# Dot products over gathered expert rows: the token operand read from an SBUF copy instead of PSUM

## The reference, cut to what matters

```python
def block(args):                       # a block of 128 tokens
    xb, ib, gb = args
    ug = expert_u[ib]                  # (128 tokens, 128 picks, 1024)
    act = jax.nn.gelu(jnp.einsum("td,tkd->tk", xb, ug)) * gb
    vg = expert_v[ib]
    return jnp.einsum("tk,tkd->td", act, vg)
out = lax.map(block, (nf.reshape(4, 128, d), idx..., gates...))
```

## Time and profile before

| | |
|---|---|
| time, median of 3 runs | 3375.94 us (3371.97 to 3378.84) |
| span of the profiled execution | 3379.1 us |
| mean granted TensorE clock | 0.910 |
| PE busy | 2796.1 us, 83% |
| POOL busy | 2040.5 us, 60% |
| DVE busy | 1395.5 us, 41% |
| ScalarE busy | 646.1 us, 19% |
| HBM read | 717.02 MB |
| software (POOL-issued) DMA queue | 587.27 MB |

### The profile page before, as it was taken

How to read it: one execution, slowest core, us unless ns; L and a number is a source line. 1 busy time by engine, 2 the same in 40 slices (tenths; PEclk the granted TensorE clock), 3 DMA queues, 4 the chain that set the end, 5 groups by cost and what they waited for, 6 DMA issues and landing times.

```text
span 3379.1 us, 27308 instructions
## 1 busy us (share of the span) xinstructions
PE 2796.1 (83%) x8913; PEld 1653.4 (49%) x8913; DVE 1395.5 (41%) x2949; ACT 646.1 (19%) x1281; POOL 2040.5 (60%) x1452
## 2 busy tenths in 40 slices
PE   7358989877777777777778699899999768899997
PEld 5234534333223323333333366568878534668876
DVE  3631565666666666666524511421110326221111
ACT  3020222221111111111112311411110323121101
POOL 4886366677777677767748683135555283345652
PEclk9688999998999899989989798899999897899999
DMA  2043599999999999999984252013322250123221
GB/s 96 31 143 99 211 369 355 375 409 399 409 409 409 392 409 409 409 388 409 409 316 155 76 174 75 25 62 99 99 89 86 70 166 33 38 75 99 95 95 59
DMA packets 294802, 720.36 MB, mean 213 GB/s; under 512 B 24821, under 2 KB 149667, under 8 KB 294707
## 3 DMA queue, kind: packets, MB, share of 16 engines
q0 software_dynamic: 160512, 587.27, 44.8%
q1 hardware_dynamic: 134194, 131.92, 12.2%
HBM read 717.02 MB, written 2.10 MB: 213 GB/s over the span
## 4 chain that ended last, share of the span: by engine, by line
PE 60%; DMA 12%; POOL 12%; DVE 7%; issue 6%; ACT 3%; DVEq 0%; ACTq 0%; SPq 0%; POOLq 0%
PE ps L731 11%; PE ps L553 9%; PE ps L556 9%; PE ps L560 9%; DMA arena<-in_expert_u_dram,arena 8%; POOL arena L1110 7%; PE ps L504 5%; PE ps L697 3%; PE ps L603 3%; POOL work L1110 2%; PE ps L826 2%; POOL whi_in L1080 2%; PE ps L515 2%; DMA arena<-in_expert_v_dram,arena 1%; DVE nT L1597 1%
## 5 line engine op out<-in xcount | busy, mean ns | idle before, releaser
L731 PE MATMUL ps<-arena 128*128 128x512 f32 x1536 | 767.6, 646 | 248.7 <-ACT arena L1337 164.0
L731 PEld LDWEIGHTS ps<-arena 128*128 128x128 f32 x1536 | 304.6, 206 | 690.6 <-issue 556.7
L1864 DVE CUSTOM_DVE_ANT_0 arena<-arena,ps 128x1024 f32<-128x1024 f32 x384 | 467.5, 1219 | 304.4 <-DMA arena<-in_expert_u_dram,arena 295.4
L1110 POOL DMA_INDIRECT arena<-in_expert_v_dram,arena x384 | 360.4, 939 | 194.9 <-PE ps L731 103.4
L1110 POOL DMA_INDIRECT arena<-in_expert_u_dram,arena x384 | 362.3, 944 | 147.2 <-issue 100.0
L1080 POOL TENSOR_SCALAR whi_f<-wring 128x2048 fp32r<-128x2048 f32 (+1 forms) x60 | 125.4, 2089 | 329.7 <-DMA wring<-in_ffn_w_in_dram 202.8
L1084 POOL TENSOR_TENSOR wlo<-wring,whi_f 128x2048 fp32r<-128x2048 f32 (+1 forms) x60 | 302.1, 5035 | 11.0 <-POOL whi_f L1080 11.0
L731 PE MATMUL ps<-work,arena 128*128 128x512 f32 x512 | 240.2, 602 | 28.5 <-DMA work<-in_expert_v_dram,arena 28.5
L556 PE MATMUL ps<-n_hi,wlo 128*128 128x512 f32 x1024 | 259.3, 396 | 3.6 <-POOL wlo L1084 3.5
L556 PEld LDWEIGHTS ps<-n_hi,wlo 128*128 128x128 f32 x1024 | 196.0, 192 | 48.1 <-POOL wlo L1084 6.0
L2046 DVE TENSOR_TENSOR arena<-ps,arena 128x512 f32 x44 | 30.4, 692 | 408.0 <-PE ps L560 408.0
(11 more groups left out here) (290 smaller groups left out, 3747.1 us busy)
## 6 DMA issues: line engine op xcount, KB each, us to landing
arena<-in_ada_w_dram POOLq DMA_DIRECT2D x48, 1024.0 KB, 6.0
wring<-in_ffn_w_in_dram SPq DMA_DIRECT2D x44, 1024.0 KB, 5.1
wring<-in_ffn_w_out_dram SPq DMA_DIRECT2D x16, 1408.0 KB, 6.2
wring<-in_gla_w_in_dram SPq DMA_DIRECT2D x12, 1024.0 KB, 5.4
wring<-in_w_in_dram SPq DMA_DIRECT2D x9, 1024.0 KB, 5.1
wring<-in_w_q_dram SPq DMA_DIRECT2D x8, 1024.0 KB, 9.7
arena<-in_expert_u_dram,arena POOLq DMA_INDIRECT x384, 9.8
arena<-in_expert_v_dram,arena POOLq DMA_INDIRECT x384, 9.9
```

The source lines that it names most:

```text
L731: mm = e.matmul(ps[:, 6 + q, :], diag[:, k, :], slot_of(s)[:, q * 512:(q + 1) * 512], start=(n % HEADS == 0 and k == 0), stop=last)
L1110: e.indirect_dma_start(slot_of(seq), None, table, bass.IndirectOffsetOnAxis(ap=idx_flat[:, n * TOPK + k:n * TOPK + k + 1], axis=0)).then_i ...
L1864: inc(e.tensor_tensor_reduce(slot_of(s), slot_of(s), ps[:, 4:6, :].rearrange("p a k -> p (a k)"), 1.0, 0.0, ALU.mult, ALU.add, dots[:, n % ...
```

## The change

`tokens(t)` of PE is now followed by a step of the same name on ScalarE: one activation (Copy) of 128x1024 from PSUM banks 4 and 5 into `row[:, 0:2, :]`. It waits for the transposes (new semaphore `x_turned`) and, from block 1 on, for the last dot of the block before (`u_used` at 128 t), and its end is `x_ready`. ScalarE does it for block 0 behind the first scores, and for the later blocks behind the gelu of the last unit of the block before. PE's transposes wait only for the copy before them (`x_ready` at t). The dots read `row` in SBUF in place of PSUM. There are still 512 dots and 32 transposes; four copies are new.

```diff
             def tokens(t):                       # PE
                 if t:
-                    need("u_used", PER_BLOCK * t)
+                    need("x_ready", t)
                 for k in range(DC):
                     mm = e.transpose(ps[:, 4 + k // 4, (k % 4) * P:(k % 4 + 1) * P], nT[:, k, t * P:(t + 1) * P], ident[:])
-                inc(mm, "x_ready")
+                inc(mm, "x_turned")
...
+            def tokens(t):                       # ScalarE
+
+                need("x_turned", t + 1)
+                if t:
+                    need("u_used", PER_BLOCK * t)
+                inc(e.activation(row[:, 0:2, :].rearrange("p a k -> p (a k)"), ps[:, 4:6, :].rearrange("p a k -> p (a k)"),
+                                 ACT.Copy), "x_ready")
+
             for h in range(WQ_FIRST):
                 wq_evac(h)
                 sc_evac(h)
+                if h == 0:
+                    tokens(0)
                 if h % 2:
                     gate_exp(h // 2)
             for n in range(UNITS):
                 if n + AHEAD < UNITS:
                     gate_exp(n + AHEAD)
                 hidden(n)
+                if n % HEADS == HEADS - 1 and n < UNITS - 1:
+                    tokens(n // HEADS + 1)
                 diagonals(n)
...
                 e.wait_ge(row_landed[s % RING], 16 * (s // RING + 1))      # DVE, u_row
-                inc(e.tensor_tensor_reduce(slot_of(s), slot_of(s), ps[:, 4:6, :].rearrange("p a k -> p (a k)"), 1.0, 0.0,
+                inc(e.tensor_tensor_reduce(slot_of(s), slot_of(s), row[:, 0:2, :].rearrange("p a k -> p (a k)"), 1.0, 0.0,
                                            ALU.mult, ALU.add, dots[:, n % 2, k:k + 1]), "u_used")
```

More of the change, by code:

```diff
@@ L88 @@
         "rot_done rope_read rope_ready angle_ready trig_ready att_s att_m att_p att_n att_t att_pt  att_o att_oh "
-        "att_oe fin_t fin_ready out_done glr_in hid_ready ada_ch ada_cols gr_ready go_chunk norm_chunk nhi_ready nlo_ready w_hi w_lo hid_raw hid_hi_ready").split()
+        "att_oe fin_t fin_ready out_done glr_in hid_ready ada_ch ada_cols gr_ready go_chunk norm_chunk nhi_ready nlo_ready w_hi w_lo hid_raw hid_hi_ready x_turned").split()
 def build(nc, A, out):
```

## The result

| | before | changed |
|---|---|---|
| median of 20 runs | 3378.77 us | 3400.34 us |
| spread | 3339.92 us to 3386.53 us, and one outlier of 5396 | 3381.24 to 3421.05 us |
| ratio of the runs | | 1.0113, 95% interval 1.0078 to 1.0149 |
| span of the profiled execution | 3379.1 us | 3385.2 us |

What follows compares the result with a forecast made beforehand. The DMA engines were taken to set the pace at 2.56 us a pair of gathers, POOL close behind at 2.49. Held gathers +124, copy 0 and PE's wait 0, on 3375.9, gave 3500 us; range 3376 to 3620.

Steps and rivals of the forecast that it cites:

- A dot with two SBUF operands holds gathers: Expert stage: a gather whose index fetch falls inside a dot's 1.22 us waits on POOL for the dot's end.
- Rival C: Expert stage: the custom dot with two SBUF operands does not hold gathers; 3376 us, give or take 3; chance 0.12.
- POOL is the second bound, 3% behind: Expert stage: POOL needs 2.49 us a pair of gathers, leaving 0.09 us a pair spare, about 40 us in all.
- The price: Expert stage: held gathers cost two thirds of the way from 0 to +182 us, +124 us, POOL mostly out of step.
- random phase: Expert stage: fetches falling at random against dots make a pair take 2.99 us against 2.58, +172 us from 650 to 1740.
- the good order: Expert stage, low end: POOL steps with the dots, one fetch free by 0.10 us, the next held 0.08; no loss.
- The first stretch, +10: From 379 to 650 us: held gathers nearly fit into POOL's waits at unit starts; +10 us for the part not overlapping.
- The copy and the hand-over: At three block changes: ScalarE's copy starts the first dot 1.1 us later; taken as 0, without cover +3.3 us.
- PE's wait: At block changes: PE no longer waits for the last dot; the wait cost nothing, taken as 0, at most 8.9 us.
- D: At three block changes: dots start 1.9 us earlier, a gain of 5.6 us, at most 8.9; about 3368 us; chance 0.04.
- Rival E: Expert stage: every u gather is stably held to a dot's end, a pair takes 3.3 us; +304, 3680 us; chance 0.08.
- B: Expert stage: the good order holds nearly throughout, POOL often held but keeping the DMA's pace; 3376 to 3430 us; chance 0.20.

Runs made afterwards that it cites:

- e1: Changed kernel with the dots reading PSUM again, copies kept, PE also waiting for a block's last dot; 3490.29 us against 3493.41 for the kernel before, on a slower chip.
- e9: Kernel before plus one tiny POOL memset behind every gather, the control; 3407.43 us, ratio 1.0104 to the kernel before.
- e10: Changed kernel plus one tiny POOL memset behind every gather; 3552.57 us, ratio 1.0545 to the kernel before.
- e7: Changed kernel with only block 0's dots reading SBUF, the others PSUM, on a slower chip; 3510.26 us against 3508.25 for the kernel before, ratio 0.9996.
- e14: Changed kernel with only block 0's dots reading SBUF, the others PSUM, at full speed; 3378.20 us against 3376.62 for the kernel before, ratio 1.0003.
- e12: The changed kernel run again, unaltered, at full speed; 3396.82 us against 3373.69 for the kernel before, ratio 1.0034.
- e4: Changed kernel with only block 0's dots reading SBUF, the others PSUM, on a slower chip; 3490.49 us against 3493.41 for the kernel before, ratio 0.9958.
- e13: Changed kernel with dots over 768 of 1024 columns, at full speed; 3378.44 us against 3376.62 for the kernel before, ratio 1.0005.
- e2: Kernel before with transposes alternating between two PSUM bank pairs, so PE waits for nothing at block changes; 3498.81 us against 3493.41, ratio 1.0007, slower chip.
- e15: Changed kernel with only the dots of blocks 1 to 3 reading SBUF, at full speed; 3394.12 us against 3376.62 for the kernel before, ratio 1.0029.
- e3: Changed kernel with dots over 768 of 1024 columns, on a slower chip; ratio 0.9957 to the kernel before.

## Why the prediction was right in its mechanism and wrong in its size

1. *The dot's length.* Right: 1.22 us, 1225 ns by the median line.
2. *A dot with two SBUF operands holds gathers.* Right, and shown: of 490 gathers whose fetch falls into a dot, 469 are longer, up to 1985 ns; with dots from PSUM none was in the kernel before, and in e1 3 of 446, by at most 0.05 us. Rival C is refuted. That it is the reading of the indices that waits is the prediction's reading; the traces show the instant, not what the gather does at it.
3. *POOL is the second bound, 3% behind.* Right: e9, 0.08 us more per gather, costs 34 us, and in the profile before POOL's waits in blocks 1 to 3 are 39 us (about 40 was forecast).
4. *The price: "Between 0 and +182 I take two thirds".* This is the step that failed. The term of +124 us measured 22 to 38 (23 or 12 in the repeat, which is unclear). It was the hold per pair that was mis-sized: +124 us over 422 pairs, with 0.09 us of spare time in each, needs 0.38 us of holds a pair, and random phase 0.50. The trace of the changed kernel has 43 us over the 388 pairs of blocks 1 to 3, 0.11 us a pair, and 39 us of waits to put against it. The kernel kept the good order for most of the time. The order that I gave the lower end was right in its numbers (held 0.07 us for a forecast 0.08, free by 0.09 for 0.10), but I wrote that "no force brings back the good order" and that POOL "cannot make up" a slip. As I read it, two things do. First, while there is a queue at the DMA engines a held gather costs queue and not time: the landings went from 5 to 12 us behind a gather to 5.6 or 6.9. The slips ate that lead once, and it wasn't needed. Second, being held is itself what restores step: the held gather goes on at a dot's end, and as POOL's 2.49 us are under the DMA's 2.56, it stays there. Where there is no queue the formula for random phase comes nearer: for e10 it gives T = 2.64 + 1.49/T = 3.12, 0.48 us over POOL's own 2.64, and 3.03 was measured, 0.34 over the 2.69 of the control.
5. *The first stretch, +10.* Open. The times of e7 and e14 show no cost of block 0, but their intervals allow 6 and 8 us, and block 0's dots take 4 to 9 us longer in the three full-speed traces where all of them read SBUF in full (changed, e12, e14). My expectation for e4, that up to two thirds of the loss sits there, is not borne out.
6. *The copy and the hand-over.* Right: the first dot of a block came 1.05 us later behind the transposes (1.1 forecast), and no cost can be seen (e13, e14; on a slower chip e1).
7. *PE's wait.* Right: worth nothing (e2, and PE 1.9 us behind the last dot with the wait and without it). D is refuted.
8. *Rival E* never became stable; in e10, where T might have gone to it, the pair took 3.03 us and not 3.3.

B was the case that came, near the middle of its 3376 to 3430 us, with 0.20 of the chance; the forecast's own case, 3430 to 3620, did not come. That 3400 lies in the stated range is no merit of the argument, as the range took in B. The signs that I gave were mixed: holds as forecast, POOL's mean per gather 831/833 = 1.00 us and not 1.1 to 1.2, dots still 2.56 us apart by the median and not 2.8 to 3.0.

The Trainium skill (SBUF — State Buffer, Who interferes with whom) has it that VectorE with two SBUF inputs contends with a GpSimd instruction that reads SBUF. The trace agrees, for gathers, which it does not list as such: 469 held, by up to 1.05 us, beside the custom dot. Its inference that tensor_tensor does not stall software-made DMA is not borne out for indirect gathers: beside the tensor_tensor of line 1781 they take up to 0.25 us longer.

What stays open: how much each slip costs and how often one comes. The runs of the changed kernel scatter more than those of the kernel before (3347 to 3420 us in e12, 3337 to 3392 before beside it; standard deviation 20 against 12 us, in e15 15 against 6.5), as chance slips would make them, and e13 speaks for the margin; but late landings can't be switched on and off, so that they are what starts a slip is read from the timelines alone, not tested.

## What to carry to other kernels

Before moving an operand of VectorE from PSUM to SBUF, see what GpSimd does meanwhile: with two SBUF operands, the dots and sums of this case held an indirect gather whose fetch fell into them. Whether that costs is decided by how much GpSimd waits anyway: here it was 3% quicker than the DMA engines, its waits shrank by 63 us, and 86 us of holds cost 20 in the profiled execution; with POOL 3% slower the same change cost 145. Add up the holds and the waits, stage by stage, before giving a price. When two periodic streams can block each other, look for the step they fall into before averaging over random phases.

## What the runs showed of the hardware that was not expected

- An indirect gather is sensitive at one instant only, 0.13 us after its start: one held there ends 0.81 us behind the dot's end (0.805 to 0.823 in 466 cases), and the rest of its 0.94 us may lie beside a dot.
- Between two VectorE instructions back to back the waiting gather gets in: in the change's burst of dots at 392 to 395 us no hold is longer than the rest of one dot (the longest is 1.05 us).
- The 367 GB/s on some chips is no even slowing: the median distance of two dots is 2.56 us there too (e1, e2, e3, e7), with more of them late, 101 over 2.7 us in e1 against 22 in the profile before, of 383.
